# An RWKV mixer's opening work moved behind the last seven units of the projection ahead of it

## The chip, the cores and the metric

One NeuronCore of a Trainium2 chip runs the whole kernel in one launch. The metric is device microseconds from the first to the last instruction of a run; lower is better. All data is float32; large products are made of three products of split halves.

## What is computed

The reference is two models of two layers behind each other. The part that matters here is the mixer of the second model, once in layer 0 and once in layer 1 (`l`), on 512 tokens of width 1024. From one projection come r, k, v (384 wide), three low-rank inputs and the inputs of two other mixers:

```python
r, k, v, w_lo, a_lo, g_lo = _split(shift_lerp(p_a, rwkv_mu[l]), A_SLAB)
if l > 0:
    v = v + (v_first - v) * sigmoid(v0 + mv @ v2)
w = -softplus(-(w0 + tanh(w_lo) @ w2)) - 0.5
a = sigmoid(a0 + a_lo @ a2)
g = sigmoid(g_lo) @ g2
kk = k * k_k / norm(k * k_k)
k = k * (1.0 + (a - 1.0) * k_a)
y = recurrence(r, exp(-exp(w)), k, v, -kk, kk * a)
y = head_layernorm(y) * ln_w + ln_b + sum(r * k * r_k) * v
```

A sparse attention mixer takes the 128 highest scores of each query: `lax.top_k(score, topk)`.

## The kernel before, in words

The kernel is a row of stages. Within a stage every engine has its own program and waits on counters (semaphores); between stages all engines meet at a barrier. Nothing of a later stage starts before the slowest engine has ended the one ahead of it. `chain_stage` (line 901) ends in a `mix_in` part: 27 units in the order of `MIX_ORDER` (line 835), each a tile of 128 output rows by 512 tokens. I call them units 0 to 26 by their place.

For a unit TensorE does 24 matmuls of 128x128 by 512 (8 tiles of the inner dimension, three split products each; `Stream.multiply`, line 693, its matmul is L705). ScalarE makes the high half of a weight tile (`split_hi`, L682), VectorE the low half (`split_lo`, L690). There are three slots for split weights, so in its turn v ScalarE waits until unit v is done, and splits the weights of unit v+3. After that it does what else turn v asks of it. VectorE in turn v makes the low half, does selection rounds (`Select.rounds`, L2553 and L2555: the next 8 maxima, and their marking), scales unit v out of PSUM (L1538), and for r, k, v, and the low ranks shifts it by one token (L1542, L1544). `ROUNDS_HERE` (line 2531) says how many rounds turn v does from v = 13 on; 48 rounds are to be done in all, those that are left in the next stage.

Behind some units TensorE has small float32 products: behind unit 20 the head sums of the squared keys (`head_sums`), behind 23 and 24 the spreading of the norms (`spread_factor`, L1052), behind 25 the turning of the values (`turn_values`, L1061). In turn 21 ScalarE takes the square root of the norms (L1313), and in turn 26 loads the Sigmoid table (L1315).

`rwkv_stage` (line 2613) then opens with the low ranks, for each third c of 384: TensorE's products w and a (32 rows each), g (64 rows), in layer 1 also v (16 rows) (`open_ranks`, L2778); ScalarE's sigmoids (L3027, L3029, L3034), the term (a-1)k_a (L3031) and the copy of g (L3037); VectorE's scan of the decays (L3120), in layer 1 the mixing of v, then k, a and the bonus product (L3132, L3133, L3135). TensorE sums the bonus over heads (`bonus_sums`, L2785). ScalarE takes four exponentials, two at first (L3042, L3043), VectorE multiplies a, kk and k by them (L3107, L3112), and only then TensorE starts the first `scores` (L2755). What follows, up to the end of the stage, I call the body; its order is written out by hand, with selection rounds between VectorE's steps.

Of the kernel before, what the change touches and what calls it, by code (L numbers as in the profile page):

```python
# [15 lines left out]
ALU = mybir.AluOpType  # L16
# [826 lines left out]
def part_two_memory(nc, m):  # L843
# [13 lines left out]
    m.acc, m.rstd = rows[:, 2, :], rows[:, 3, :]  # L857
    hidden = behind + 40 * KB
# [42 lines left out]
def chain_stage(nc, m, d, name, what, carried=False):  # L901
# [14 lines left out]
    INDEXED, SCORED, SUMMED, TURNED = place_of[INDEX] + 2, place_of[INDEX] + 4, 20, 25  # L916
# [22 lines left out]
    with stage(nc, name, *Stream.SIGNALS, *Rms.SIGNALS, "y_hi", "y_lo", "scaled", "silu_ready", "product", "hidden",  # L939
               "hidden_hi", "hidden_lo", "out_ready", "emptied", "shifted", "own", "v_psum", "v_ready", "gated", "turn_loaded", "moved",  # L940
               "turned", "final_ready", "stored", "index_out", "index_moved", "masks_loaded", "lo_w_loaded", "iw_psum", "iw_ready",
               *(["half_done", "half_sums", "half_root", "half_factor", "half_spread", "gained", "warm"] if what[-1][0] == "final" else ()),
               "rel_psum", "rel_out", "added", "score_made", "sq_ready", "ss_psum", "ss_floor", "ss_root", "ss_factor", "kk_spread",
               "kk_made", "selector_made", "table_loaded", "lo_opened",
               "lo_ready", "mv_ready", "reset", *Select.SIGNALS,
# [31 lines left out]
        def _(pe):  # L977
# [67 lines left out]

            def spread_factor(c):
                if c == 2:
# [7 lines left out]
            def turn_values():  # L1055
                pe.wait_ge(s["kk_made"], C)
# [59 lines left out]
            for part, rms in zip(parts, norm):  # L1116
# [24 lines left out]
                elif part.kind == "mix_in":  # L1141
                    first_units(part, rms, (0, 1))
                    for u in range(2, N):
                        if u >= 6:
                            pe.wait_ge(s["emptied"], u - 5)
                        st.multiply(pe, part.u + u, u % 6, m.xs, 0, True, True)
# [13 lines left out]
                        elif u == TURNED:  # L1160
                            turn_values()

        @block.scalar
        def _(act):
            def positive(i):
# [5 lines left out]
                nc.scalar.activation(m.relu[h % 4][:, 0:n], m.ps[:, 6 + h % 2, 0:n], ACT.Relu).then_inc(s["rel_out"], 1)  # L1171

# [69 lines left out]
            for part, rms, following in zip(parts, norm, follows):  # L1242
# [28 lines left out]
                elif part.kind == "mix_in":  # L1271
                    for v in range(N):
# [27 lines left out]
                        if place_of[GATE + 1] + 1 <= v < place_of[GATE + 1] + 1 + C:  # L1300
# [3 lines left out]
                                                 scale=m.col(f"rwkv_k_k{part.layer}", c)).then_inc(s["sq_ready"], 1)  # L1304
                        if v == SUMMED - 1:
# [5 lines left out]
                        if v == SUMMED + 1:  # L1311
                            act.wait_ge(s["ss_floor"], 1)
                            nc.scalar.activation(factor, factor, ACT.Sqrt).then_inc(s["ss_root"], 1)  # L1313
                        if v == N - 1:
                            nc.scalar.activation(m.stat[:, 0:1], m.eps[:, 0:1], ACT.Sigmoid).then_inc(s["table_loaded"], 1)  # L1315

        @block.gpsimd
        def _(pool):
            if parts[-1].kind == "mix_in":
# [10 lines left out]
                nc.gpsimd.memset(m.reset.rearrange("p (n c) -> p n c", c=HD)[:, :, 0:1], 0.0).then_inc(s["reset"], 1)  # L1330

# [2455 lines left out]
```

## Time and profile before

| | us |
|---|---|
| median of 3 runs | 3702.46 |
| lowest, highest | 3695.45, 3704.89 |
| span of the profiled execution | 3696.9 |

The profiled execution's own time is not given beside its span; the span lies 5.6 us under the median of the runs. In rows of the timeline the columns are start, us, engine, line, operation, output<-inputs, and in brackets how long the engine was idle before it and what ended that. PE is TensorE's matmul, PEld its weight load, DVE VectorE, ACT ScalarE, POOL GpSimd. Where a row has xN it merges N records from that start on.

### The profile page before, as it was taken

How to read it: one execution, taken by the hardware profiler on the slowest of the kernel's cores; microseconds unless marked ns; L12 is line 12 of the kernel's file. 1: busy time of each engine (PE TensorE's matmuls, PEld its weight loads, DVE VectorE, ACT ScalarE, POOL GpSimd, SP SyncE). 2: the span in 40 equal slices, each digit the busy share in tenths (PEclk: the TensorE clock that was granted, in tenths of full speed). 3: DMA queues.
4: the chain of work that ended last, by engine and by line, in shares of the span. 5: the costliest groups of instructions: out<-in, count | busy, mean ns of one | idle time of the engine just before them, and what ended most of it. 6: DMA issues, size and time to landing. Idle time of an engine off the chain costs nothing. (4 is left out here: it accounts for less than half of the span.)

```text
span 3696.9 us, 61545 instructions
## 1 busy us (share of the span) xinstructions
PE 3586.1 (97%) x26295; PEld 3100.4 (84%) x26295; DVE 2026.3 (55%) x3385; ACT 1432.0 (39%) x2297; POOL 139.1 (4%) x189
## 2 busy tenths in 40 slices
PE   8999999899999998999999999999999999999999
PEld 8999999788899998888877678888888877668887
DVE  7667653544476635543478564444444478565443
ACT  6844332544453324332243343223222244343232
POOL 0000000011000000000003100000000002100000
PEclk9999999999999998999999999999999999999999
DMA  3232223122212232333320023333333320013332
GB/s 136 80 98 84 91 91 92 64 76 76 69 64 92 91 94 76 99 96 98 111 69 3 24 80 97 97 94 101 97 97 94 110 80 2 24 64 99 97 95 80
DMA packets 87872, 303.21 MB, mean 82 GB/s; under 512 B 9632, under 2 KB 11808, under 8 KB 87344
## 3 DMA queue, kind: packets, MB, share of 16 engines
q1 hardware_dynamic: 87600, 299.28, 25.7%
q8 instruction: 208, 3.41, 0.4%
q14 instruction: 64, 0.52, 0.0%
HBM read 297.11 MB, written 2.13 MB: 81 GB/s over the span
## 5 line engine op out<-in xcount | busy, mean ns | idle before, releaser
L690 DVE TENSOR_TENSOR two_w_lo<-one_raw,two_w_hi 128x1024 fp32r<-128x1024 f32 (+1 forms) x334 | 400.5, 1199 | 754.7 <-ACT two_w_hi L682 752.6
L705 PE MATMUL psum<-two_x_hi,two_w_hi 128*128 128x512 f32 x1768 | 694.6, 393 | 1.2 <-DVE two_rows L1488 0.9
L705 PE MATMUL psum<-two_x_hi,two_w_lo 128*128 128x512 f32 x1768 | 688.4, 389 | 0.0
L705 PE MATMUL psum<-two_x_lo,two_w_hi 128*128 128x512 f32 x1768 | 687.9, 389 | 0.0
L682 ACT CAST two_w_hi<-one_raw 128x1024 fp32r<-128x1024 f32 (+1 forms) x334 | 342.0, 1025 | 823.6 <-PE psum L705 817.1
L705 PEld LDWEIGHTS psum<-two_x_hi,two_w_hi 128*128 128x128 f32 x1768 | 331.8, 188 | 88.8 <-issue 17.8
L2286 PE MATMUL psum<-one_x_hi,one_w_hi 128*128 128x264 f32 (+1 forms) x1376 | 391.6, 285 | 7.8 <-DVE one_x_lo L790 7.3
L705 PEld LDWEIGHTS psum<-two_x_hi,two_w_lo 128*128 128x128 f32 x1768 | 331.8, 188 | 69.8
L705 PEld LDWEIGHTS psum<-two_x_lo,two_w_hi 128*128 128x128 f32 x1768 | 331.9, 188 | 69.4 <-issue 1.4
L2286 PE MATMUL psum<-one_x_lo,one_w_hi 128*128 128x264 f32 (+1 forms) x1376 | 389.4, 283 | 0.0
L2286 PE MATMUL psum<-one_x_hi,one_w_lo 128*128 128x264 f32 (+1 forms) x1376 | 389.0, 283 | 0.0
L705 PE MATMUL psum<-two_h_hi,two_w_hi 128*128 128x512 f32 x794 | 308.9, 389 | 0.0
L705 PE MATMUL psum<-two_h_hi,two_w_lo 128*128 128x512 f32 x794 | 308.9, 389 | 0.0
L705 PE MATMUL psum<-two_h_lo,two_w_hi 128*128 128x512 f32 x763 | 296.8, 389 | 0.0
L2286 PEld LDWEIGHTS psum<-one_x_hi,one_w_hi 128*128 128x128 f32 x1376 | 259.4, 189 | 10.3 <-DVE one_x_lo L790 9.6
L2286 PEld LDWEIGHTS psum<-one_x_lo,one_w_hi 128*128 128x128 f32 x1376 | 259.8, 189 | 0.0
L2286 PEld LDWEIGHTS psum<-one_x_hi,one_w_lo 128*128 128x128 f32 x1376 | 259.5, 189 | 0.0
L690 DVE TENSOR_TENSOR one_w_lo<-one_raw,one_w_hi 128x1024 fp32r<-128x1024 f32 (+2 forms) x145 | 170.6, 1179 | 124.8 <-ACT one_w_hi L682 123.0
L2286 PE MATMUL psum<-one_h_hi,one_w_hi 128*128 128x264 f32 (+1 forms) x704 | 198.9, 283 | 2.4 <-ACT one_pads L2391 2.4
L2286 PE MATMUL psum<-one_h_lo,one_w_hi 128*128 128x264 f32 (+1 forms) x704 | 199.0, 283 | 0.0
L2286 PE MATMUL psum<-one_h_hi,one_w_lo 128*128 128x264 f32 (+1 forms) x704 | 198.6, 282 | 0.0
L682 ACT CAST one_w_hi<-one_raw 128x1024 fp32r<-128x1024 f32 (+2 forms) x145 | 146.8, 1015 | 112.4 <-PE psum L2286 108.5
(540 smaller groups left out, 6723.1 us busy)
## 6 DMA issues: line engine op xcount, KB each, us to landing
one_raw<-in_swi_in SPq DMA_DIRECT2D x172, 512.0 KB, 3.5
one_raw<-in_ffn_in SPq DMA_DIRECT2D x88, 512.0 KB, 3.6
one_raw<-in_swi_out SPq DMA_DIRECT2D x64, 448.0 KB, 3.2
one_raw<-in_mix_in SPq DMA_DIRECT2D x54, 512.0 KB, 3.5
one_raw<-in_attn_w SPq DMA_DIRECT2D x32, 512.0 KB, 3.8
one_raw<-in_swi_out SPq DMA_DIRECT2D x32, 512.0 KB, 3.5
one_raw<-in_ffn_out SPq DMA_DIRECT2D x32, 448.0 KB, 3.3
one_raw<-in_lru_w SPq DMA_DIRECT2D x24, 512.0 KB, 5.3
```

Source lines behind the costliest of these rows:

```text
L682: self.nc.scalar.copy(self.place(u)[0], self.m.raw[:, u % self.RAW, 0:self.cols(u)]).then_inc(self.s["w_hi"], 1)
L690: self.nc.vector.tensor_tensor(lo, self.m.raw[:, u % self.RAW, 0:self.cols(u)], hi.bitcast(FP32), ALU.subtract).then_inc(self.s["w_lo"], 1)
L705: last = self.nc.tensor.matmul(self.m.ps[:, bank, :], a[:, w], b[:, k0 + k, :], start=(start and k == 0 and q == 0), stop=(stop and k == n ...
L2286: ins = nc.tensor.matmul(m.ps[:, bank + h, skip:HALF], a[:, w], b[:, k0 + k, h * HALF + skip:(h + 1) * HALF], start=(start and q == 0), st ...
```

## The change

The opening moves into `chain_stage`. Its products go behind units 20 to 25 in pairs, through two PSUM banks (4 and 5); the units from 20 on use banks 2, 3, 0 and 1. `turn_values` goes from behind unit 25 to behind unit 21. ScalarE takes a pair in the turn after it, and scales r by r_k in turn 24. VectorE's scans and scaled keys are in its turns 23 to 25. GpSimd mixes v (layer 1) and makes the bonus product, in both layers. The mixer's stage then begins with the exponentials and the bonus sums. Five selection rounds go from the chain into the mixer's body. Buffers are placed anew.

```diff
-    INDEXED, SCORED, SUMMED, TURNED = place_of[INDEX] + 2, place_of[INDEX] + 4, 20, 25
+    INDEXED, SCORED, SUMMED, TURNED = place_of[INDEX] + 2, place_of[INDEX] + 4, 20, 21
...
+    w, OPENED = Rwkv(m), 20
+    pairs = [pair for c in range(C) for pair in (((c, "w"), (c, "a")), ((c, "v"), (c, "g")) if LW else ((c, "g"),))]
+    opens = [one for pair in pairs for one in pair]
+    opened_as = {one: n + 1 for n, one in enumerate(opens)}
+    unit_bank = lambda v: v % 6 if v < OPENED else (2, 3, 0, 1)[(v - OPENED) % 4]
...
+            def open_ranks(pair):
+                for c, kind in pair:
+                    n = opened_as[c, kind] - 1
+                    if n >= 2:
+                        pe.wait_ge(s["z_out"], n - 1)
...
+                    nc.tensor.matmul(m.ps[:, 4 + n % 2, :], w.lo_w[lo:lo + rows, at + c * P:at + (c + 1) * P],
+                                     right[lo:lo + rows, :], start=True, stop=True).then_inc(s["z_psum"], 1)
...
-                            pe.wait_ge(s["emptied"], u - 5)
+                            pe.wait_ge(s["emptied"], u - (5 if u < OPENED + 2 else 3))
...
-                        elif u == TURNED:
+                        if OPENED <= u < OPENED + len(pairs):
+                            open_ranks(pairs[u - OPENED])
+                        if u == TURNED:
                             turn_values()
...
+            def take_opened(pair, layer):
...
+                    act.wait_ge(s["z_psum"], n)
+                    if kind == "w":
+                        nc.scalar.activation(w.cum[:, c, :], z, ACT.Sigmoid, bias=col("w0")).then_inc(s["z_out"], 1)
...
+                        elif v == OPENED + 4:
+                            act.wait_ge(s["shifted"], NR)
...
                         if v == SUMMED + 1:
                             act.wait_ge(s["ss_floor"], 1)
                             nc.scalar.activation(factor, factor, ACT.Sqrt).then_inc(s["ss_root"], 1)
+                        if OPENED < v <= OPENED + len(pairs):
+                            take_opened(pairs[v - OPENED - 1], part.layer)
                         if v == N - 1:
-                            nc.scalar.activation(m.stat[:, 0:1], m.eps[:, 0:1], ACT.Sigmoid).then_inc(s["table_loaded"], 1)
+                            nc.scalar.activation(m.stat[:, 0:1], m.eps[:, 0:1], ACT.Exp).then_inc(s["table_loaded"], 1)
...
+                for c in range(C):
+                    if LW:
...
+                        nc.gpsimd.tensor_tensor(rest, rest, v, ALU.subtract).then_inc(s["mixed"], 1)
...
+                        nc.gpsimd.tensor_tensor(rest, rest, w.sv[c], ALU.mult).then_inc(s["mixed"], 1)
...
+                        nc.gpsimd.tensor_tensor(v, v, rest, ALU.add).then_inc(s["mixed"], 1)
+                    pool.wait_ge(s["r_gained"], c + 1)
+                    pool.wait_ge(s["keyed"], 2 * c + 1)
+                    nc.gpsimd.tensor_tensor(w.prod[c], w.gained_r[c], w.k[:, c, :], ALU.mult).then_inc(s["prod_ready"], 1)
...
+            def key_terms(c):
+                k, a = w.k[:, c, :], w.a[:, c, :]
+                dve.wait_ge(s["z_out"], opened_as[c, "w"])
+                nc.vector.tensor_tensor_scan(w.cum[:, c, :], m.reset, w.cum[:, c, :], 0.0, ALU.mult, ALU.add).then_inc(
...
-ROUNDS_HERE = (1, 1, 1, 1, 1, 1, 1, 1, 1, 1, 2, 3, 4, 3)
+ROUNDS_HERE = (1, 1, 1, 3, 2, 1, 1, 1, 1, 1, 0, 1, 1, 2)
...
-                select.rounds(dve, 1, hold=0 in lanes)
+                select.rounds(dve, 3 if 0 in lanes else 2, hold=0 in lanes)
...
-                select.rounds(dve, 2 if 0 in lanes else 1, hold=0 in lanes)
+                select.rounds(dve, 3 if 0 in lanes else 2, hold=0 in lanes)
```

How the order of instructions moves is shown at two places. The first is ScalarE from turn 20 on in layer 0. L1313 before and L1374 now are the same square root; L1211, L1213 and L1215 are the sigmoid of w, the sigmoid of a and the term (a-1)k_a. Before:

```order
L682 CAST two_w_hi<-one_raw 128x1024 x2
L1313 ACT_TABLE_LOAD
L1313 ACTIVATE two_work<-two_work 96x512
L682 CAST two_w_hi<-one_raw 128x1024 x2
L1315 ACT_TABLE_LOAD
L1315 ACTIVATE stat<-eps 128x1
```

And now:

```order
L682 CAST two_w_hi<-one_raw 128x1024 x2
L1374 ACT_TABLE_LOAD
L1374 ACTIVATE two_work<-two_work 96x512
L1211 ACT_TABLE_LOAD
L1211 ACTIVATE two_rows<-psum,vectors 128x512
L1213 ACTIVATE two_other<-psum,vectors 128x512
L1215 ACTIVATE two_wide<-two_other,stat,vectors 128x512
L682 CAST two_w_hi<-one_raw 128x1024
L1220 COPY two_other<-psum 128x512
L682 CAST two_w_hi<-one_raw 128x1024
L1211 ACTIVATE two_rows<-psum,vectors 128x512
```

The first pair stands behind the weights of turns 20 and 21, the square root and a second table load; the copy of the first g (L1220) behind the weights of turn 22.

The second place is TensorE in layer 1, now, where unit 21 ends and unit 22 begins. L1071 is `open_ranks` (here v and g of the first third), L1091 `turn_values`:

```order
L705 MATMUL psum<-two_x_hi,two_w_lo 128x512
L1071 MATMUL psum<-two_wide 128x512
L1071 MATMUL psum<-two_low,two_wide 128x512
L1091 MATMUL psum<-identity,two_misc 128x128 x8
L705 MATMUL psum<-two_x_hi,two_w_hi 128x512
```

Before, the matmuls of units 21 and 22 followed each other directly, and the eight transposes stood behind unit 25.

## Rows read from the trace of the kernel before

**Rows 1.** The page: the span, and its part 1, busy time of each engine.
```profile
span 3696.9 us, 61545 instructions
...
PE 3586.1 (97%) x26295; PEld 3100.4 (84%) x26295; DVE 2026.3 (55%) x3385; ACT 1432.0 (39%) x2297; POOL 139.1 (4%) x189
```

**Rows 2.** Windows by stage, layer 0 and layer 1; columns in the first row.
```profile
core 0: us, PE busy (x) PEld busy (x) DVE busy (x) ACT busy (x) POOL busy (x), PEclk, DMA share, GB/s
...
1928.68:1964.70 36.02, 36.02 (x160) 28.22 (x158) 34.37 (x67) 6.78 (x8) 0.64 (x2) 1.00 0.00 1
...
1964.70:1967.13 2.43, 0.39 (x2) 0.00 (x1) 2.07 (x5) 0.00 (x0) 0.00 (x0) 1.00 0.00 0
...
1967.13:1981.22 14.09, 14.06 (x24) 4.27 (x25) 11.56 (x16) 11.38 (x17) 1.46 (x1) 0.64 0.00 0
...
1981.22:2071.70 90.48, 80.91 (x2893) 76.58 (x2893) 64.45 (x143) 36.59 (x80) 32.53 (x31) 1.00 0.06 21
...
3083.57:3103.72 20.15, 20.08 (x30) 6.00 (x31) 17.63 (x25) 13.43 (x20) 0.00 (x0) 0.58 0.00 0
```

**Rows 3.** Timeline, TensorE, around the end of unit 23: start us, us, instruction.
```profile
1944.92 0.39 PE L705 MATMUL psum<-two_x_hi,two_w_lo 128*128 128x512 f32 x1
...
1945.24 1.13 PE L1052 MATMUL psum<-two_work 2*128 2x512 f32 x4
...
1946.30 0.50 PE L705 MATMUL psum<-two_x_hi,two_w_hi 128*128 128x512 f32 x1
```

**Rows 4.** Timeline, ScalarE and VectorE, the projection's units 21 to 26, layer 0.
```profile
1934.52 1.05 ACT L682 CAST two_w_hi<-one_raw 128x1024 fp32r<-128x1024 f32 x1 [5.60 <-PE psum L705]
...
1935.59 1.28 ACT L1313 ACT_TABLE_LOAD   x1
...
1936.88 0.63 ACT L1313 ACTIVATE two_work<-two_work 96x512 f32<-96x512 f32 x1
...
1939.96 1.05 ACT L682 CAST two_w_hi<-one_raw 128x1024 fp32r<-128x1024 f32 x1 [2.45 <-PE psum L705]
...
1945.40 1.05 ACT L682 CAST two_w_hi<-one_raw 128x1024 fp32r<-128x1024 f32 x1 [4.39 <-PE psum L705]
...
1966.16 0.68 DVE L1538 TENSOR_TENSOR two_other<-psum,two_rows 128x512 f32<-128x512 f32 x1
```

**Rows 5.** Timeline, the mixer's opening in layer 0, up to the first scores.
```profile
1967.13 0.33 PEld L2778 LDWEIGHTS psum<-two_low,two_wide 32*128 32x128 f32 x4 [2.46 <-issue]
...
1968.35 0.69 ACT L3027 ACTIVATE two_high<-psum,vectors 128x512 f32<-128x512 f32 x1 [20.39 <-PE psum L2778]
...
1978.41 0.84 ACT L3042 ACTIVATE two_high<-two_high 128x768 f32<-128x768 f32 x1
...
1981.22 0.47 PEld L2755 LDWEIGHTS psum<-two_ring,two_wide 64*64 64x64 f32 x24 [0.90 <-issue]
```

**Rows 6.** Timeline, TensorE, the same opening in layer 1.
```profile
3083.60 1.13 PE L2778 MATMUL psum<-two_low,two_wide 32*128 32x512 f32 x4 [2.07 <-PEq L89]
...
3084.57 1.02 PE L2778 MATMUL psum<-two_wide 16*128 16x512 f32 x2
...
3085.52 0.69 PE L2778 MATMUL psum<-two_low,two_wide 64*128 64x512 f32 x1
```

**Rows 7.** Timeline, VectorE: selection rounds, and its shortest wait in the body where rounds are added.
```profile
1957.18 0.55 DVE L2553 MAX8 two_keys<-two_keys 128x8 f32<-128x384 f32 x1
...
1958.42 0.56 DVE L2553 MAX8 two_keys<-two_keys 128x8 f32<-128x384 f32 x1
...
2012.67 1.26 DVE L3104 TENSOR_TENSOR two_work<-psum,two_work 128x384 f32<-128x384 f32 x2 [1.76 <-PE psum L2748]
```

**Rows 8.** Timeline, GpSimd: one product of 128 by 512.
```profile
3124.20 2.50 POOL L2711 TENSOR_TENSOR two_ring<-two_ring,two_low 128x512 f32<-128x512 f32 x2
```

**Rows 9.** Timeline and windows, TensorE at the start of the next stage's projection.
```profile
3287.31 0.47 PE L705 MATMUL psum<-two_h_hi,two_ahead_hi 128*128 128x512 f32 x1 [2.59 <-DVE two_h_lo L1449]
...
3287.30:3291.20 3.90, 3.89 (x10) 3.10 (x11) 3.90 (x7) 3.90 (x8) 0.00 (x0) 0.56 0.95 379
```

More of the change, by code:

```diff
@@ L857, in part_two_memory @@
     m.acc, m.rstd = rows[:, 2, :], rows[:, 3, :]
+    m.decays = rows[:, 0:3, :]
     hidden = behind + 40 * KB
@@ L1511, in _ @@
                     own.wait()
+                    at = COLS[f"rwkv_k_a{part.layer}"][0]
+                    nc.vector.tensor_scalar(minus_k_a, m.vec[:, at:at + C], -1.0, None, ALU.mult).then_inc(s["minus_ready"], 1)
                     for v, unit in enumerate(MIX_ORDER):
@@ L2588, in __init__ @@
         self.lo = low[:, 3 * N:3 * N + SEQ]
-        self.el = at(high, 0)
-        self.logw, self.cum, self.prev = at(high, N), at(high, 2 * N), at(high, 3 * N)
-        self.a, self.g, self.bonus = at(ring, 0), at(ring, N), at(ring, 2 * N)
-        self.neg = self.logw
-        self.sv = self.prev
-        self.prod = [ring[:, 4 * N + j * SEQ:4 * N + (j + 1) * SEQ] for j in range(3)]
+        self.cum, self.a = m.decays, m.other[:, 4:7, :]
+        self.g = [m.other[:, 8, :], m.other[:, 15, :], m.values[1]]
+        self.sv = [m.work[:, 6, 0:SEQ], m.work[:, 7, 0:SEQ], m.other[:, 7, :]]
+        self.prod = [wide[:, 6 * SEQ:7 * SEQ], wide[:, 7 * SEQ:8 * SEQ], m.work[:, 3, 0:SEQ]]
+        self.gained_r = [m.work[:, c, 0:SEQ] for c in range(3)]
+        self.neg = at(high, N)
+        self.el, self.bonus = at(ring, 0), at(ring, 2 * N)
         self.kk = at(wide, 0)
@@ L2601, in __init__ @@
         slots = (cut(high, N, 15) + cut(ring, 3 * N, 9) + cut(wide, N, 6) + cut(work, 0, 11)
[L2602 removed]
+                 + cut(m.y[:, :, :].rearrange("p a b -> p (a b)"), 0, 10) + cut(ring, N, 4) + cut(m.reset, 0, 1)
+                 + cut(low, 3 * N, 1))
         take = lambda n: [slots.pop(0) for _ in range(n)]
@@ L2659, in rwkv_stage @@
     chunks_first = lambda x: x.rearrange("p n c i -> p c n i")
-    with stage(nc, f"rwkv{layer}", "z_psum", "z_out", "cum_ready", "exp_out", "less_one", "prod_ready", "bonus_psum",
-               "bonus_out", "bonus_ready", "own", "halved", "v_turned", "b_turned", "k_turned", "a_turned", "tok_v", "tok_b", "tok_k", "tok_a",
+    with stage(nc, f"rwkv{layer}", "exp_out", "bonus_psum", "bonus_out", "bonus_ready", "halved", "v_turned", "b_turned", "k_turned", "a_turned", "tok_v", "tok_b", "tok_k", "tok_a",
                "ab_ba", "ab_out", "ak_rb", "rk", "low", "edges", "up", "one_added", "MAK", "MRB", "MRK", "g1", "h1", "z1", "g2",
@@ L2769, in to_tokens, with bonus_sums @@
                 return last
-            def open_ranks():
+            def bonus_sums():
                 for c in range(C):
-                    for n, (q, kind) in enumerate(opened):
-                        if c == 2:
-                            pe.wait_ge(s["z_out"], n + 1)
-                        lo, rows, at = {"w": (0, 32, 0), "a": (32, 32, 0), "g": (64, 64, 0), "v": (32, 16, 384)}[kind]
-                        right = w.mv if kind == "v" else w.lo
-                        nc.tensor.matmul(z_bank(c, q), w.lo_w[lo:lo + rows, at + c * P:at + (c + 1) * P], right[lo:lo + rows, :],
-                                         start=True, stop=True).then_inc(s["z_psum"], 1)
-            def bonus_sums():
-                pe.wait_ge(s["z_out"], 2 * NZ)
-                for c in range(C):
-                    pe.wait_ge(s["prod_ready"], c + 1)
                     nc.tensor.matmul(m.ps[:, BONUS_BANK[c], :], m.head_ones, w.prod[c], start=True, stop=True).then_inc(
@@ L3516, in _ @@
                 pool.wait_ge(s["boosted"], c + 1)
-                nc.gpsimd.tensor_tensor(m.y[:, c, 0:SEQ], y, w.g[:, c, :], ALU.mult).then_inc(s["done"], 1)
+                nc.gpsimd.tensor_tensor(m.y[:, c, 0:SEQ], y, w.g[c], ALU.mult).then_inc(s["done"], 1)
         @block.vector
```

120 lines of the change are left out of this document (62 added, 58 removed).

## The prediction

> **What bounds the kernel now.** I began with the page: the span is 3696.9 us, and TensorE's matmuls are busy for 97% of it [rows 1]. Nothing but TensorE's own queue, or a stretch where it stands still, sets the end. The windows by stage then show where the change acts [rows 2]. In the last seven units of layer 0's projection TensorE is busy all the time at the full clock (1.00, the 2.4 GHz level). From the last matmul's start to the next stage 2.43 us pass. Then the opening takes 14.09 us in layer 0 and 20.15 us in layer 1, at a mean clock of 0.64 and 0.58: most of it ran at 1.2 GHz. Its busy PE is thin work, few rows high. So both openings lie wholly on the path. Whatever goes behind the units instead must not stop TensorE there, where it is the bound.
>
> The timeline gives the clockwork of a unit. A unit's last matmul starts at 1944.92, the small float32 product behind it at 1945.24, and the next unit at 1946.30 [rows 3]. So a small product costs 1.06 us. With T for the start of a unit's last matmul, the next unit starts at T+1.38; without such a product it starts at T+0.23, one matmul's pitch (a unit of 24 takes 5.44 us, the distance of two weight splits [rows 4]). ScalarE's split of a weight tile starts at T+0.48 (1945.40 against 1944.92), after ScalarE has been idle for 2.45 to 5.60 us waiting for TensorE to end exactly that unit [rows 4]. This wait is the key to the change: in turn v nothing that ScalarE has behind its split can start before unit v is done.
>
> **What is removed.** The exponentials start at 1978.41 and the scores at 1981.22, 2.81 us later [rows 5]. They now open the stage. Three bonus products fit beside them, if 1.06 us each is not much too low; I take 2.85 us for the whole opening. That saves 14.09 - 2.85 = 11.2 us in layer 0 and 20.15 - 2.85 = 17.3 us in layer 1. The stage's end also moves up: VectorE scaled the last unit only at 1966.16, behind three selection rounds, while TensorE's last matmul had started at 1964.70 [rows 2, 4]. With five rounds fewer it should start at T+0.5, and 0.68 us of it and the 0.3 us of the barrier lead to T+1.5, in place of T+2.43: 0.9 us in each layer. Together 30.3 us.
>
> **What is added to TensorE.** w and a, each 32 rows high, start together and cost one step: v starts 0.97 us after them and g 0.95 us after v [rows 6]. So in layer 0 six steps are added, in layer 1 nine, of about 1 us each. This would leave a gain of some 14 us, if TensorE never waited.
>
> **What TensorE now waits for.** Only two banks take these products. The third product waits until ScalarE has emptied the first one's bank, the fourth until the second is emptied, and so on, and TensorE stands still with everything behind it, the next unit first. I go through the units, layer 0.
> - Behind 20: w and a of the first third, behind the head sums. No wait: +1.1 us.
> - Behind 21: g waits for the sigmoid of w. ScalarE reaches it in turn 21, after the split (T+0.48), a table load which started 1.07 us behind the split's start and took 1.28 us, the root (0.63 us) [rows 4], a second load for the Sigmoid (the same 1.28 us) and the sigmoid itself (0.69 us [rows 5]). That is T + 0.48 + 1.07 + 1.29 + 0.63 + 1.28 + 0.69 = T+5.44. Then g (1.06 us) and the transposes (about 1 us, moved here from behind 25). Unit 22 starts at T+7.65 in place of T+0.23: +7.4 us.
> - Behind 22: a of the second third needs g's bank. Split until T+1.53, copy of g below 0.69 us: T+2.2, then 1.06 us, so T+3.25 in place of T+0.23: +3.0 us.
> - Behind 23: g needs the second w taken, again T+2.2, then 1.06 us: T+3.3 in place of T+1.38: +1.9 us.
> - Behind 24: ScalarE has no more splits, and has caught up: +1.0 us. Behind 25: g in place of the transposes: +0.1 us.
>
> The sum is 14.5 us for layer 0. In layer 1 v is added to g. Behind 21 this is a step more (+8.4); behind 22 a waits for the copy of g that follows the sigmoid of v (T+2.8, +3.6); behind 23 g comes after v (T+4.2, +2.9); 24 +1.0; 25 +1.1; with the 1.1 of unit 20 it is 18.1 us. Both layers: 32.6 us added against 30.3 us saved, +2.3 us.
>
> **The table load** deserves a second look, since two stand in the long wait. The trace shows 1.28 us, and the root starts 0.01 us behind its end; the split before it ended 0.02 us ahead of it [rows 4]. The Trainium skill, in "ScalarE: Activation LUTs", section "What ACT_TABLE_LOAD costs", counts a drain of about 1.38 us on top of each switch, 2.66 us in all. By that rule each wait behind unit 21 would be 2.8 us longer, 5.5 us over both layers, and the forecast 3715. Here the rows have no room for such a drain, so I go by the row.
>
> **The clock.** TensorE now stands still from about T+0.5 to T+5.4 behind unit 21, and then runs three thin products. The rows show what a still stretch does: after 2.59 us of idleness the next unit's matmuls ran at 0.56, ten of them in 3.9 us [rows 9], where the pitch of 0.23 us would have let in 17. A clock of 0.56 over 3.9 us is 3.4 us at half speed, which costs 1.7 us of work. The idle time here is twice that one, so I count one such stretch in each layer, and a third for the waits behind 22 and 23 of layer 1, where only thin work runs for some 4 us: 5.1 us. The bounds are 0 (the clock falls and returns while TensorE is idle) and about 14 us (eight stretches). The opening itself lost its clock before; its new form has two thirds of its time filled with full-height products, and I leave it at no change.
>
> **What is hidden.** VectorE has 11.56 us of busy time in the old opening of layer 0 [rows 2], about eight of which now lie in turns 23 to 25. Those turns get longer by the waits, and lose eight rounds (1.24 us each, from 1957.18 to 1958.42 [rows 7]); VectorE is ready for the last unit. The five rounds that enter the body go where VectorE waits: the shortest of these waits is 1.76 us [rows 7], for one round of 1.24 us. I cost them at nothing; without that cover it would be 5 x 1.24 = 6.2 us in a layer. Two and one more rounds in turns 16 and 17 delay nothing that TensorE waits for, since weights are split three units ahead. GpSimd's products take 1.25 us each (two in 2.50 [rows 8]). The last chain in layer 1 is mix, mix, bonus, 3.8 us from the last sigmoid of v at about T+2.2 of unit 25. It ends at T+6, and unit 26 is scaled by T+8.9: hidden by 2.9 us.
>
> **Sum.** +2.3 + 5.1 = +7.4 us on the profiled execution, 3704.3 us of span. The median of the runs lies 5.6 us above that span, so the forecast is 3702.5 + 7.4 = 3710 us, 0.2% slower. A measurement of this kernel tells about 0.3% from no change, 11 us: I call it the same.
>
> **Rivals.**
> 1. *TensorE doesn't wait* (faster). The work moves behind the units as meant and ScalarE is in time. Then 30.3 us are saved and 16 us added: 3688 us. For it: ScalarE is busy for only 6.78 of 36.02 us there [rows 2]. Against it: its idle time lies ahead of the split, not behind it [rows 4], and the order puts the first sigmoid behind a split and two table loads. Chance 0.12, which takes in a mixed case with half of the waits gone, 3697 us.
> 2. *The clock stays low* (slower). Waits behind 21, 22 and 23 in both layers, with only thin products in between, keep TensorE at 1.2 GHz through units 22 to 24, as thin products went with a clock of 0.64 and 0.58 in the old openings [rows 2]. Each further stretch costs 1.7 us. The case decides against "same" from the sixth stretch on (2.3 + 6 x 1.7 = 12.5); with eight it is 3702.5 + 2.3 + 13.6 = 3718 us. The Trainium skill says in "TensorE: Matmul & The Clock Gate", section "What's actually happening", that the slow state is the default and that activity releases it, which speaks for this rival. Chance 0.18.
> 3. *The drain of a table switch* as the skill's rule has it, 3715 us. Chance 0.05.
> 4. *Rounds or GpSimd appear on the path*: a round in each of the four places of the body not covered, or GpSimd late for the barrier, 3 to 6 us: 3715 us. Chance 0.05.
> 5. *The change doesn't do what it says*: the order shows all of it in place, with the same number of table loads; I give it nothing.
>
> **Numbers.** My case holds 0.60. Faster by over 0.3% (under 3691) has 0.11, slower by over 0.3% (over 3713.6) 0.26, the rest, 0.63, is the same. The range goes from 3696 (no lost clock, and half of a wait less) to 3720 (the second rival).
>
> **What would show it.** In the new profile each layer should have TensorE idle for about 5 us behind unit 21 until the first sigmoid ends, and for about 1 us behind 22 and 23. The projection's tail should be some 14.5 and 18 us longer, each followed by units with a clock of 0.5. The opening should be 2.8 to 3 us, the body unchanged at 90.5 us in layer 0 [rows 2]. It is wrong if TensorE runs through unit 21's end without a wait, if the opening takes over 4 us, or if the body gets longer.

## The result, and the profile after

| | before | after |
|---|---|---|
| median, us | 3704.89 (9 runs) | 3716.12 (9 runs) |
| lowest to highest, us | 3695.45 to 3711.45 | 3713.53 to 3719.84 |
| ratio after / before | | 1.0033, 95% interval 1.0025 to 1.0041 |
| profiled execution: time, span | span 3696.9 | 3717.87, span 3715.8 |

The kernel became 11.2 us slower by the medians, 0.33% by the ratio. A second set of runs of the same two kernels gave 1.0036 (1.0024 to 1.0048). Both intervals leave out 1, so the change is small but real. The time lies inside the predicted range (3696 to 3720) and on the slow side of the forecast (3710 us). It also lies above 3713.6 us, from where the prediction counted "slower" (chance 0.26) and no longer "the same" (0.63). From the median of the kernel before in this larger set that line of 0.3% stands at 3716.0 us, and the kernel after is on it.

The two profiled spans differ by 18.9 us, more than the medians. The profile of before comes from the low end of its times. What is compared below is therefore measured inside the stages that the change touches. A second profile of before, span 3697.8 us, repeats its openings and tails within 0.2 us; against a second profile of after, span 3711.3 us, it differs by 13.5 us.

The windows by stage, kernel before, cut anew so that they fit the kernel after: from the start of the head sums behind unit 20 to the end of the last unit (the tail), and from there to the first score product (barrier and opening). Layer 0, then layer 1.

```profile
core 0: us, PE busy (x) PEld busy (x) DVE busy (x) ACT busy (x) POOL busy (x), PEclk, DMA share, GB/s
1927.71:1965.09 37.38, 37.38 (x165) 28.32 (x164) 34.95 (x69) 7.59 (x8) 0.64 (x2) 1.00 0.00 1
1965.09:1981.25 16.16, 14.08 (x26) 4.30 (x25) 13.30 (x20) 11.38 (x17) 1.46 (x1) 0.68 0.00 0
3044.16:3081.54 37.38, 37.38 (x165) 28.32 (x164) 35.86 (x70) 7.59 (x8) 0.64 (x2) 1.00 0.00 1
3081.54:3103.75 22.21, 20.09 (x31) 6.03 (x31) 19.37 (x29) 13.46 (x21) 0.00 (x0) 0.62 0.00 0
```

The same view, kernel after; the third row is layer 0's body, from the first score product to the next stage.

```profile
1929.70:1984.88 55.18, 48.70 (x183) 32.62 (x182) 35.10 (x56) 18.40 (x24) 5.45 (x5) 0.91 0.00 0
1984.88:1989.78 4.90, 2.81 (x6) 1.06 (x6) 3.69 (x4) 3.19 (x5) 1.46 (x1) 1.00 0.00 0
1989.78:2081.71 91.93, 80.98 (x2893) 76.56 (x2893) 70.29 (x158) 36.17 (x79) 32.56 (x31) 1.00 0.06 20
3052.60:3116.33 63.73, 56.09 (x189) 36.22 (x188) 37.12 (x57) 20.24 (x27) 17.68 (x14) 0.84 0.00 1
3116.33:3120.12 3.79, 2.75 (x7) 1.06 (x7) 2.58 (x4) 2.60 (x4) 0.00 (x0) 1.00 0.00 0
```

These rows hold most of the account; they answer to [rows 2]. The openings, barrier included, shrank as meant: 16.16 to 4.90 us and 22.21 to 3.79 us, 29.7 us saved. The tails grew from 37.38 us to 55.18 and 63.73 us, 44.2 us added. The net is +14.5 us in this profile (+13.0 us in a second one). Of the 18.9 us between the spans another 2.3 us lie in the two bodies (91.93 and 91.27 us, for 90.47 us in both layers before), and some 2 us elsewhere; neither was followed up. PE busy tells how: of the 55.18 us of layer 0's tail only 48.70 are busy, so 6.5 us are idle. And the mean clock, which was 1.00, is 0.91 and 0.84; the records of the granted clock behind these means give 10.2 us at half speed in layer 0's tail, in three stretches of 3.4 us, and 20.5 us, six stretches, in layer 1's.

The waits of TensorE in these tails: what it waited for, us in all, times, the longest. Kernel after, layer 0 (first two rows) and layer 1.

```profile
PE psum L1071 <- ACT two_rows L1211: 5.9, 2, 5.1
PE psum L1071 <- ACT two_other L1220: 0.6, 1, 0.6
...
PE psum L1071 <- ACT two_work L1218: 1.8, 1, 1.8
```

L1071 is the opened product, L1211 ScalarE's sigmoid of w; layer 1 has the row on L1211 word for word as layer 0 has it. The timeline shows the place. TensorE, layer 0, units 21 to 23 of the kernel after (columns as in [rows 3]):

```profile
1937.07 0.39 PE L705 MATMUL psum<-two_x_hi,two_w_lo 128*128 128x512 f32 x1
1942.59 2.07 PE L1071 MATMUL psum<-two_low,two_wide 64*128 64x512 f32 x2 [5.13 <-ACT two_rows L1211]
1944.59 1.97 PE L1091 MATMUL psum<-identity,two_misc 128*128 128x128 f32 x8
1946.21 0.78 PE L705 MATMUL psum<-two_x_hi,two_w_hi 128*128 128x512 f32 x1
...
1952.70 1.12 PE L1071 MATMUL psum<-two_low,two_wide 32*128 32x512 f32 x2
1954.44 1.12 PE L1071 MATMUL psum<-two_low,two_wide 32*128 32x512 f32 x2 [0.62 <-ACT two_other L1220]
...
1963.00 1.12 PE L1071 MATMUL psum<-two_low,two_wide 64*128 64x512 f32 x2 [0.72 <-ACT two_rows L1211]
...
1971.35 0.69 PE L1082 MATMUL psum<-two_work 2*128 2x512 f32 x1
1971.36 0.70 PE L1071 MATMUL psum<-two_low,two_wide 32*128 32x512 f32 x2
```

ScalarE beside it, turn 21 of layer 1 (the same to 0.03 us in layer 0); the unit's last matmul started at 3059.97:

```profile
3060.45 1.04 ACT L682 CAST two_w_hi<-one_raw 128x1024 fp32r<-128x1024 f32 x1 [6.64 <-PE psum L705]
3061.51 1.28 ACT L1374 ACT_TABLE_LOAD   x1
3062.81 0.63 ACT L1374 ACTIVATE two_work<-two_work 96x512 f32<-96x512 f32 x1
3063.45 1.28 ACT L1211 ACT_TABLE_LOAD   x1
3064.75 0.69 ACT L1211 ACTIVATE two_rows<-psum,vectors 128x512 f32<-128x512 f32 x1
```

The sigmoid ends at T+5.47; the prediction had T+5.44. Each table load is followed by its operation 0.01 to 0.02 us later, as in [rows 4], so the drain that the Trainium skill counts in "ScalarE: Activation LUTs", section "What ACT_TABLE_LOAD costs", takes no time here. Its 3715 us is near the measured time for another reason.

Then look at what follows the wait: g took 2.07 us and the transposes 1.97 us, where the same product took 1.12 us behind unit 23. They ran at half clock, 1.2 GHz, as the matmuls behind the idle time in [rows 9] had. The distances between the last matmuls of successive units measure wait and clock together (taken from the start of each unit's last matmul on TensorE's timeline; the predicted ones have no clock term):

| from unit to unit | before | predicted, layer 0 | after, layer 0 | predicted, layer 1 | after, layer 1 |
|---|---|---|---|---|---|
| 20 to 21 | 6.64 | 7.7 | 7.69 | 7.7 | 7.69 |
| 21 to 22 | 5.44 | 12.8 | 15.31 | 13.8 | 18.04 |
| 22 to 23 | 5.44 | 8.4 | 8.46 | 9.0 | 12.23 |
| 23 to 24 | 6.72 | 8.6 | 10.19 | 9.6 | 11.20 |
| 24 to 25 | 6.72 | 7.7 | 6.73 | 7.7 | 6.73 |
| 25 to 26 | 6.34 | 6.4 | 6.73 | 7.4 | 7.77 |

("Before" has 17.52 us for units 20 to 23 together, shared out here by its pattern, 6.64 for a unit behind a small product and 5.44 for one without.) Where the clock was full, the predicted distances hold within 0.4 us, with one exception: behind unit 24 the w and a products ran side by side with the spread product (1971.35 and 1971.36 above), and that step cost nothing. Where the clock fell, the excess is 2.5 and 1.6 us in layer 0 and 4.2, 3.2 and 1.6 us in layer 1: 13.1 us. The prediction had 5.1 us for all of it.

The clock did not stay low from one unit to the next. Windows of layer 1, kernel after: the rest of unit 22 and the wait behind it, the start of unit 23, and the end of unit 23 with what stands behind it:

```profile
3074.50:3081.10 6.60, 4.82 (x20) 3.42 (x20) 1.53 (x2) 2.11 (x3) 0.83 (x1) 1.00 0.00 0
3081.30:3088.00 6.70, 6.70 (x16) 4.63 (x15) 3.49 (x7) 0.00 (x0) 1.90 (x2) 0.50 0.00 0
3088.20:3094.80 6.60, 5.88 (x20) 2.85 (x19) 3.00 (x4) 4.05 (x6) 0.00 (x0) 1.00 0.01 1
```

The clock came back to 1.00 behind each loss, and was lost again behind the next unit.

### The profile page after: what moved, and what is told of

It reads as the page before. It is cut to its first block and busy times, and to the rows that moved or that the text cites. A ratio compares the mean times of both kernels' runs of the same rounds, so it can differ in the third digit from the quotient of the medians.

```text
span 3715.8 us, 61554 instructions
## 1 busy us (share of the span) xinstructions
PE 3588.6 (97%) x26295; PEld 3106.4 (84%) x26295; DVE 2019.3 (54%) x3370; ACT 1438.7 (39%) x2303; POOL 161.0 (4%) x204
```

## The experiments

Each kernel starts from the kernel after, unless the text says otherwise. All ratios are to the kernel before.

**The kernel after again, and what is hidden.** First the two controls.

> The changed kernel again, beside the others on one chip: ratio 1.003, with half-speed stretches behind units 21 and 23 in layer 0 and 21, 22 and 23 in layer 1. If these stretches lie elsewhere, their place is chance and not the work before them.

Measured: 3714.10 us, 1.0036 (1.0024 to 1.0048). Tails 53.65 and 63.82 us, openings 4.90 and 3.79 us. Layer 1 has the half clock behind units 21, 22 and 23 again. In layer 0 it lasts 6.8 us in place of 10.2 us, the stretch behind unit 23 is missing, and the tail is 1.5 us shorter. So one such stretch of 3.4 us costs about 1.5 us, and whether it comes can change from one run to the next. Layer 1 again has six stretches, but one behind unit 22 and two behind unit 23, where the first profile has two and one.

```diff
 # kernel before, the rounds alone
-ROUNDS_HERE = (1, 1, 1, 1, 1, 1, 1, 1, 1, 1, 2, 3, 4, 3)
+ROUNDS_HERE = (1, 1, 1, 3, 2, 1, 1, 1, 1, 1, 0, 1, 1, 2)
...
-                select.rounds(dve, 1, hold=0 in lanes)
+                select.rounds(dve, 3 if 0 in lanes else 2, hold=0 in lanes)
...
-                select.rounds(dve, 2 if 0 in lanes else 1, hold=0 in lanes)
+                select.rounds(dve, 3 if 0 in lanes else 2, hold=0 in lanes)
```

> The kernel before with the new places of the selection rounds alone (five rounds later, in the body of the mixer). Theory 1, as predicted: they are hidden in both places, 3704 us, ratio 1.000, layer 0's body at 90.5 us. Theory 2 (they lie on the path in the body): five rounds of 1.2 us in either layer, 3710 us or more.

Measured: 3701.42 us, 0.9997 (0.9988 to 1.0006). The rounds are hidden in both places. Layer 0's body, first score to first mean product, took 91.09 us, against 90.47 and 91.77 us in the two profiles of the kernel before: its length varies by over a microsecond with no change at all. Two things came with it. Each mixer's stage starts 1.0 us earlier behind the last matmul (TensorE waits 1.05 us there, for 2.07 us before), since VectorE has a round less in the last turn. So 2.0 of the 29.7 us saved in the openings come from the moved rounds alone. And the opening of layer 0 ran at a mean clock of 0.90 in this profile, with 3.0 us at half speed in place of 10.2 us. With the barrier it took 14.74 us, against 16.16 us; without it 13.69 us, against 14.09 us. 7.2 us more at half clock thus cost it only 0.4 us. That the rest of its length is the chain on ScalarE and VectorE fits this, but was not tried.

**The wait taken away.** This is the main experiment.

```diff
                     for v in range(N):
...
+                        if v == OPENED + 1:
+                            act.wait_ge(s["added"], len(heads))
+                            act.wait_ge(s["minus_ready"], 1)
+                            if LW:
+                                act.wait_ge(s["mv_ready"], 1)
+                        elif v == OPENED + 2:
+                            act.wait_ge(s["v_psum"], 1)
+                        if OPENED < v <= OPENED + 3:
+                            take_opened(pairs[v - OPENED - 1], part.layer)
                         st.split_hi(act, u + v + 4)
...
-                        if OPENED < v <= OPENED + len(pairs):
+                        if OPENED + 3 < v <= OPENED + len(pairs):
                             take_opened(pairs[v - OPENED - 1], part.layer)
```

The same waits stood behind the split before; they move with the call.

> ScalarE takes the opened pairs of turns 21, 22 and 23 ahead of its weight split, so that it no longer waits for the unit's last matmul before the first sigmoid. Theory 1 (the waits for z_out and the half clock behind them are what keeps the change from gaining): the waits of 5.13, 0.62 and 0.72 us in layer 0 and 5.13, 1.78 and 0.72 us in layer 1 go, 14.1 us; with them goes part of the 14 us that the half clock costs in the two tails. 3702 us if the clock stays as it is, 3690 us if most of its stretches go: a ratio to the kernel before of 0.996 to 0.999. Theory 2 (the thin products by themselves lower the clock, the wait does not matter to it): 3702 to 3704 us, with as many half-speed stretches as in the changed kernel. Theory 3 (another engine is late as well, the wait only hid it): within 3 us of 3716 us, with a new releaser behind unit 21.

> take_first once more beside it, for the interval of its gain: 3685 us, ratio 0.996, tails of 43.3 and 47.9 us, layer 0's opening 1.1 us longer than with the early copy.

Measured: 3685.22 us, 0.9961 (0.9949 to 0.9973), and the second time 3688.99 us, 0.9963 (0.9949 to 0.9976): 12 to 18 us faster than the kernel before, some 29 us faster than the kernel after. Windows, kernel take_first, layer 0 and layer 1:

```profile
1928.47:1971.78 43.31, 43.31 (x183) 29.58 (x182) 34.96 (x56) 19.67 (x25) 5.44 (x5) 1.00 0.00 0
1971.78:1976.68 4.90, 2.82 (x7) 1.06 (x7) 3.69 (x4) 3.19 (x5) 1.46 (x1) 1.00 0.00 0
3040.00:3087.85 47.85, 47.85 (x189) 31.68 (x188) 37.12 (x57) 21.58 (x28) 17.35 (x14) 0.96 0.00 1
3087.85:3091.64 3.79, 2.74 (x6) 1.06 (x7) 2.58 (x4) 2.60 (x4) 0.00 (x0) 1.00 0.00 0
```

PE busy equals the window again: TensorE never waits in either tail. The number of operations is that of the kernel after; ScalarE has one table load more in each layer (25 and 28 operations for 24 and 27). ScalarE in turn 21, layer 0, where the unit's last matmul started at 1935.84:

```profile
1930.66 1.28 ACT L1211 ACT_TABLE_LOAD   x1 [0.98 <-PE psum L1071]
1935.47 0.69 ACT L1211 ACTIVATE two_rows<-psum,vectors 128x512 f32<-128x512 f32 x1 [3.52 <-DVE two_keys L1422]
1936.05 0.68 ACT L1213 ACTIVATE two_other<-psum,vectors 128x512 f32<-128x512 f32 x1
1936.77 0.81 ACT L1215 ACTIVATE two_wide<-two_other,stat,vectors 128x512 f32<-128x512 f32 x1
1937.49 1.04 ACT L682 CAST two_w_hi<-one_raw 128x1024 fp32r<-128x1024 f32 x1
```

The table load now lies in idle time, and the bank is empty at 1936.16, when g would start: just in time, since the sigmoid first waits for VectorE's last score sum. The tails fell by 11.9 and 15.9 us, 27.8 us in all. Of that 14.1 us are the waits. Of the other 13.7 us, 1.1 us are a step behind unit 22 of layer 0. There w and a stand together now, where in the kernel after w ran alone and a only behind the wait (1952.70 and 1954.44 above):

```profile
1943.75 1.13 PE L1071 MATMUL psum<-two_low,two_wide 32*128 32x512 f32 x4
```

The last 12.6 us are clock: of 10.2 and 20.5 us at half speed in the two tails only 3.4 us in layer 1 are left, the same stretch in the profiles of take_first_again and take_first_copy. Theory 1 holds in its stronger form, with most stretches gone and 3690 us expected; theory 3 falls, and theory 2 holds for that one stretch only.

**The clock taken back, the wait left.** 22 dense products stand in the wait behind unit 21.

```diff
+                        if u == OPENED + 1:
+                            for _ in range(22):
+                                nc.tensor.matmul(m.ps[:, 7, :], m.xs.hi[:, 0, 0:P], m.xs.hi[:, 0, :], start=True, stop=True)
                         if OPENED <= u < OPENED + len(pairs):
                             open_ranks(pairs[u - OPENED])
```

> The wait behind unit 21 stays, but TensorE spends it in 22 dense 128x512 products into bank 7, whose result nobody reads (22 x 0.227 = 5.0 us of the 5.13 us wait). Theory 1 (the idle stretch behind unit 21 lowers the clock for what follows): the g product, the v product, the eight transposes and the first matmuls of unit 22 run at full clock, 2.5 us less in layer 0 and 4.4 us less in layer 1, some 3709 us. Theory 2 (the clock falls from the thin products, whatever stands before them): 3716 us, the same stretches at half speed. Theory 3 (the fill itself delays the product behind it): 3718 us or more.

Measured: 3708.96 us, 1.0022 (1.0013 to 1.0031); tails 52.62 and 57.93 us at a clock of 0.97 and 0.94. TensorE, layer 0:

```profile
1937.64 0.39 PE L705 MATMUL psum<-two_x_hi,two_w_lo 128*128 128x512 f32 x1
1937.87 5.15 PE L1192 MATMUL psum<-two_x_hi 128*128 128x512 f32 x22
1943.17 1.12 PE L1071 MATMUL psum<-two_low,two_wide 64*128 64x512 f32 x2 [0.16 <-ACT two_rows L1214]
1944.23 1.09 PE L1091 MATMUL psum<-identity,two_misc 128*128 128x128 f32 x8
```

The same g product starts no earlier behind its unit, but takes 1.12 us for 2.07, the transposes 1.09 for 1.97. Unit 21 to 22 is now 12.77 and 13.83 us, the 12.8 and 13.8 us that the prediction had without the clock. So behind unit 21 the idle stretch is what lowers the clock, and dense products in its place, even useless ones, hold it. The shorter waits behind 22 and 23 are still there, and one stretch is left in layer 0 and two in layer 1, for three and six. 8.4 us came back inside the tails. This profile's whole span (3715.5 us) shows less of it than the median: it has 110 us at half speed outside the two tails, the profile of the kernel after 91 us.

**Half of the wait.** The sigmoid before the root, both still behind the split.

```diff
+                        if OPENED < v <= OPENED + len(pairs):
+                            take_opened(pairs[v - OPENED - 1], part.layer)
                         if v == SUMMED + 1:
                             act.wait_ge(s["ss_floor"], 1)
                             nc.scalar.activation(factor, factor, ACT.Sqrt).then_inc(s["ss_root"], 1)
-                        if OPENED < v <= OPENED + len(pairs):
-                            take_opened(pairs[v - OPENED - 1], part.layer)
```

> The changed kernel with one pair of steps on ScalarE swapped in turn 21: behind its split it takes the first opened pair at once, and the square root with its table load (0.63 and 1.28 us) comes after it. Theory 1 (the wait behind unit 21 is ScalarE's chain ahead of the first sigmoid, piece by piece): the wait of 5.13 us becomes 3.2 us in both layers, nothing else moves, the clock falls as before: 3.8 us less, 3711 us. Theory 2 (a shorter idle time also spares half-speed time, in proportion): 3706 us. Theory 3 (the square root, now some 5 us later, holds back VectorE's reciprocal of 3.34 us and the spread behind unit 23): 3716 us or more, with a wait for the reciprocal behind unit 23.

Measured: 3714.20 us, 1.0032 (1.0021 to 1.0043), no gain. The waits of TensorE in the two tails, kernel root_last, layer 0 (first two rows) and layer 1:

```profile
PE psum L1071 <- ACT two_rows L1211: 5.3, 2, 3.2
PE psum L1071 <- ACT two_other L1220: 0.6, 1, 0.6
...
PE psum L1071 <- ACT two_rows L1211: 3.9, 2, 3.2
PE psum L1071 <- ACT two_work L1218: 3.2, 1, 3.2
```

The wait behind unit 21 is 3.2 us, to the tenth. But the table that the root leaves behind must be changed back, and that load now stands before the next sigmoid: in turn 22 in layer 1 (1.8 us became 3.2) and in turn 23 in layer 0 (0.7 became 2.1). In layer 1:

```profile
3079.72 1.04 ACT L682 CAST two_w_hi<-one_raw 128x1024 fp32r<-128x1024 f32 x1 [8.66 <-PE psum L705]
3080.78 1.28 ACT L1218 ACT_TABLE_LOAD   x1
3082.08 0.69 ACT L1218 ACTIVATE two_work<-psum,vectors 128x512 f32<-128x512 f32 x1
```

In all the waits fell only from 14.1 to 13.0 us. The first half of theory 1 is right, its "nothing else moves" is wrong, and my reason for theory 3 is wrong too: VectorE was not late. The half-speed time in the tails was 10.2 and 17.1 us, against 10.2 and 20.5 us in the kernel after: the shorter wait spared one stretch at most, and nothing in proportion (theory 2).

**The other way round.** ScalarE as in the kernel after, and TensorE asks later.

```diff
-                        st.multiply(pe, part.u + u, unit_bank(u), m.xs, 0, True, True)
+                        if u > OPENED + 1:
+                            st.multiply(pe, part.u + u, unit_bank(u), m.xs, 0, True, False, None, (0, 6))
+                            open_ranks(pairs[u - OPENED - 1])
+                            st.multiply(pe, part.u + u, unit_bank(u), m.xs, 0, False, True, None, (6, 8))
+                        else:
+                            st.multiply(pe, part.u + u, unit_bank(u), m.xs, 0, True, True)
...
-                        if OPENED <= u < OPENED + len(pairs):
-                            open_ranks(pairs[u - OPENED])
+                        if u == OPENED:
+                            open_ranks(pairs[0])
```

> The order on ScalarE stays as in the changed kernel; instead TensorE issues pairs 1 to 5 of the opened products six eighths into the next unit, 4.1 us and more of dense products later than before. Theory 1 (what costs is that TensorE asks for a bank before ScalarE, behind its split and two table loads, has emptied it): the waits of 5.13, 0.62 and 0.72 us in layer 0 and 5.13, 1.78 and 0.72 us in layer 1 shrink to 1 us or less, and the half clock behind them goes: 3690 us, as with take_first. Theory 2 (ScalarE's late take is on the path in another way too, for VectorE or the stage's end): over 3700 us, and a wait at the last units or the stage's opening. Theory 3 (thin products in the middle of a unit cost more than at its end): 1 us more for each of ten pairs, 3700 us.

Measured: 3691.29 us, 0.9971 (0.9962 to 0.9980). Windows: both tails, and layer 1's opening.

```profile
1929.65:1974.70 45.05, 44.98 (x183) 29.63 (x182) 35.10 (x56) 17.98 (x23) 5.46 (x5) 1.00 0.00 0
3042.21:3090.40 48.19, 48.11 (x189) 30.51 (x188) 36.70 (x57) 19.94 (x26) 15.36 (x13) 1.00 0.00 1
3090.40:3095.59 5.19, 2.75 (x8) 1.06 (x7) 2.59 (x4) 3.15 (x6) 2.09 (x2) 1.00 0.00 0
```

The waits are gone and the clock is 1.00 in both tails. So it is the order of ask and take that counts, not which engine moves. A small part of theory 2 shows: in layer 1 the last v product comes later, GpSimd's chain behind it ends at 3092.48, and the stage starts 1.4 us later than in take_first. Layer 0's tail is 1.7 us longer than take_first's, for all five moved pairs, not 1 us each as theory 3 had it. About 1.1 us of it is the spread product of unit 24, which has no w and a beside it any more. In layer 1 the tail is 0.3 us longer, without take_first's stretch of half speed.

**More thin work, without a wait.** take_first, with each opened product issued twice.

```diff
-                    nc.tensor.matmul(m.ps[:, 4 + n % 2, :], w.lo_w[lo:lo + rows, at + c * P:at + (c + 1) * P],
-                                     right[lo:lo + rows, :], start=True, stop=True).then_inc(s["z_psum"], 1)
+                    for twice in range(2):
+                        last = nc.tensor.matmul(m.ps[:, 4 + n % 2, :], w.lo_w[lo:lo + rows, at + c * P:at + (c + 1) * P],
+                                                right[lo:lo + rows, :], start=True, stop=True)
+                    last.then_inc(s["z_psum"], 1)
```

> As take_first, but each of the opened products is issued twice into the same bank (the second result is the same). Theory 1 (a step of opened products costs about 1.05 us of TensorE at full clock, where two of different rows share it, as the sum had it, and the clock falls behind an idle TensorE, not behind thin products): some 6 steps in layer 0 and 9 in layer 1 more at 1.05 us each, 15 us, 3700 us, and no more half-speed stretches in the tails than take_first's one. Theory 2 (thin products by themselves lower the clock): another 3 or more stretches of 3.4 us at half speed in the two tails, 3705 us or more. Theory 3 (the small products overlap with what stands next to them): under 3690 us.

Measured: 3705.94 us, 1.0008 (0.9999 to 1.0016). Tails:

```profile
1924.54:1972.99 48.45, 48.45 (x201) 31.91 (x200) 35.11 (x56) 19.78 (x25) 5.46 (x5) 1.00 0.00 0
3046.35:3106.78 60.43, 60.42 (x213) 38.17 (x212) 35.99 (x57) 21.72 (x28) 16.63 (x14) 0.89 0.00 1
```

Layer 0 is as theory 1 had it, at a clock of 1.00: 5.1 us for six steps, 0.86 us for each in place of 1.05. Layer 1 is as theory 2 had it: 12.6 us for nine steps, with three more stretches at half speed than take_first. TensorE is busy all the time there, and the clock fell inside or right behind the three rows of thin products of some 5 us (from 3054.9, 3074.4 and 3094.0 on). So TensorE lost the clock in these runs behind idle time, and also without any, where thin products stood in a long row.

**Two small things.** GpSimd's copy of layer 0's values is taken out of the opening, and issued piece by piece behind the projection.

```diff
-            if not LW:
-                nc.gpsimd.tensor_copy(m.v_first[:, :, :], w.v).then_inc(s["bonus_ready"], 1)
...
                 for c in range(C):
+                    if not LW:
+                        pool.wait_ge(s["shifted"], SHIFTED.index(2 * C + c) + 1)
+                        nc.gpsimd.tensor_copy(m.v_first[:, c, :], w.v[:, c, :])
...
-                        act.wait_ge(s["bonus_ready"], C + (not LW))
+                        act.wait_ge(s["bonus_ready"], C)
```

> As take_first, and GpSimd's copy of the values of layer 0 (1.46 us, beside the opening's first VectorE product) is done in three pieces before the stage begins, behind the projection. Theory 1 (VectorE's product of keys by decay took 2.09 us in layer 0 instead of 0.96 us because the copy ran beside it): it takes 0.96 us now, layer 0's opening is 1.1 us shorter, 3684 us, which the times cannot tell from take_first's 3685 us, but the trace can. Theory 2 (the product is long for another reason, its operand or its place behind the stage's start): it stays at 2.1 us.

Measured: 3684.85 us, 0.9954 (0.9942 to 0.9966). VectorE's product of keys by decay, first in take_first, then in take_first_copy:

```profile
1973.68 2.08 DVE L3165 TENSOR_TENSOR two_other<-two_other,two_high 128x768 f32<-128x768 f32 x1 [1.17 <-ACT two_high L3100]
```

```profile
1973.93 0.96 DVE L3166 TENSOR_TENSOR two_other<-two_other,two_high 128x768 f32<-128x768 f32 x1 [1.17 <-ACT two_high L3101]
```

The opening is 3.79 us, as in layer 1. This version has the lowest median, although its time can't be told from take_first's.

In the last one the fourth pair of products is moved from behind the spreads of unit 23 into the middle of unit 24, on top of take_first_copy.

> As take_first_copy, but the fourth pair of opened products (behind the two spreads of unit 23, and in layer 1 three products long together) is issued in the middle of unit 24 instead, so that thin products stand apart. Theory 1 (the one half-speed stretch left in layer 1's tail, at 3066 us, follows 3.0 us of thin products in a row): it goes, 1.5 us less there, layer 1's tail 46.3 us instead of 47.85 us, layer 0's tail unchanged at 43.3 us, 3683 us. Theory 2 (the thin products count together wherever they stand in these units): the stretch stays, perhaps later, 47.8 us. Theory 3 (ScalarE takes the fourth pair too late for the fifth): a wait of TensorE of 1 us or more behind unit 24 in either layer.

Measured: 3689.39 us, 0.9967 (0.9955 to 0.9980), the same as take_first beside it. Tails 43.56 and 46.68 us, no wait; layer 1 has no half-speed stretch in its tail any more, where the three profiles with the pair behind unit 23 all had one. That is as theory 1 had it, but it is one profile, and 1.2 us is too little for the times to show.

> The kernel before once more, for a second profile of its openings: the first profile lay near the low end of its times. If the difference between its profiled span and its median lies in the two openings, their half-speed time differs from the 10.2 and 17.1 us of the first profile; if not, the openings repeat within 1 us and the difference lies in the rest of the kernel.

Measured: 3699.61 us, a single run. Its openings, cut as above, took 16.33 and 22.21 us, at half clock for 10.2 and 17.1 us, as in the first profile. Both profiles are from the low end of the times. Why runs of the kernel before spread over 16 us stays open. The openings are an unlikely place, since in rounds_only 7.2 us less at half clock made one only 0.4 us shorter.

## Why the prediction held, and which term was off

- **The key step held.** "Nothing that ScalarE has behind its split can start before unit v is done": the wait behind unit 21 is 5.13 us in both layers, its chain ends at T+5.47 for a predicted T+5.44, and turning the order around on either engine removes it.
- **The removed work** was put at 30.3 us and measured 29.7 us, of which the moved rounds alone give 2.0 us. The stage starts at T+1.44, for a predicted T+1.5. The opening was put at 2.85 us; it is 2.75 us in layer 1 and 3.85 us in layer 0, because GpSimd's copy ran beside VectorE's product; without the copy there it was 2.74 us. The prediction had named that copy nowhere. It cost 1.1 us.
- **The added work without the clock** was put at 32.6 us. Measured it is 44.2 - 13.1 = 31.1 us, the difference being mostly the step behind unit 24 that cost nothing. The start of unit 22 in layer 0, T+7.65, is 0.15 us more than its own terms give (5.44 + 1.06 + 1); in filled, at full clock, it is T+7.44. The first rival, that TensorE doesn't wait, was priced right: 16 us added and 3688 us. take_first removes the waits, and has tails 16.4 us longer than before and 3685 and 3689 us.
- **The clock was the term that was off**: "I count one such stretch in each layer, and a third", 5.1 us. There were three stretches in layer 0 and six in layer 1. They cost 13.1 us by the table of distances, and 12.6 us by take_first, which still has one of them. That is near the upper bound the text gave (14 us). The count came from the idle time behind unit 21 alone. What I missed was to follow my own sum: behind unit 21 of layer 1 stand 3.0 us of thin products at full speed (as in take_first), and 5.6 us at the half speed that the wait brought; behind unit 22 stands a wait of 1.8 us and a product, behind 23 the spreads, a wait and two more. Each of these places lost the clock anew.
- **The second rival** had the size, eight stretches and 3718 us, but not the course: it had TensorE at 1.2 GHz through units 22 to 24, while the clock came back behind each loss. How many stretches one wait brings stays open; the profiles differ in it from run to run.
- **The range held in part by luck.** The main case, +7.4 us, is half of the +14.5 and +13.0 us found in place. The measured time is inside the range because its upper end was set by the second rival.
- The clock rule that the prediction took from the Trainium skill, "TensorE: Matmul & The Clock Gate", section "What's actually happening", agrees with filled: with activity in the wait's place the clock held there. It does not tell how doubled lost the clock in layer 1, with TensorE busy for 60.42 of 60.43 us.
- **Hidden work stayed hidden.** Rounds alone: 0.9997. VectorE and GpSimd release TensorE nowhere in the tails. The body, put at 90.5 us, took 91.9 us in layer 0 (91.6 us in the second profile), and 90.5 and 91.8 us in two profiles of the kernel before. The prediction had called a longer body a sign of being wrong; here it is 1.5 us longer, where the two profiles of the kernel before differ by 1.3 us.
- **Against the median** the sum is +7.4 us predicted, +11.2 us measured, while the profile shows +14.5 us in place. The medians thus show less than the profiles; the reference median had also moved from 3702.46 to 3704.89 us with more runs.

## What to carry to other kernels

Work moved off a serial opening into the gaps of a bound engine paid here only once the bound engine no longer asked before the helper could have answered. With two banks, compare when the helper is free for the first take with when the third product is issued, and put the take ahead of whatever waits for the bound engine, or ask later. Price the wait with the clock that it costs: here 14.1 us of waiting came with some 13 us lost to half speed. A table switch that is ordered away from one wait turns up at the next use of the other table; look where it lands before counting it as saved. A third PSUM bank for these products, another way to keep TensorE from waiting, was not tried.

## What the runs showed of the hardware that was not expected

- GpSimd's 1.46-us copy of 128x1536 float32 beside a VectorE product of 128x768 made that product take 2.09 us in place of 0.96 us. The same product took 0.96 us when the copy was moved away. GpSimd's own products of 128x512 took from 1.26 to 1.67 us in the tails; what VectorE did beside them was not varied.
- The spread product, 2 rows high, and the w and a products, 32 rows each, ran side by side where they were issued next to each other (1971.35 and 1971.36 us above). The spreads of unit 23 and the g product behind them, 64 rows high, did not overlap even in take_first, where g did not wait (1.13 us from 1950.47 on, then 1.12 us from 1951.53 on).
- Dense products that nobody needs (22 in 5.15 us) held the clock at 2.4 GHz through a wait, and made the kernel 5 to 7 us faster than the kernel after by the medians.
- In layer 1 of doubled TensorE was busy for 60.42 of 60.43 us, and still ran 13.7 us at 1.2 GHz.
